# LoRA products of the RWKV group in one pass over 96 stacked rows, issued before the norm of kk

## What is computed

```
p = p + (token_shift(p) - p) * mu
r, k, v, wl, al = jnp.split(p, [G, 2 * G, 3 * G, 3 * G + L], axis=-1)
decay = jnp.exp(-RWKV_DECAY_SCALE * jax.nn.sigmoid(w0 + jnp.tanh(wl) @ w2))
a = jax.nn.sigmoid(a0 + al @ a2)
kk = (k * k_k).reshape(B, T, H, N).astype(jnp.float32)
kk = kk / jnp.maximum(jnp.sqrt(jnp.sum(kk * kk, axis=-1, keepdims=True)), 1e-12)
k = k * (1.0 + (a - 1.0) * k_a)
```

## Time and profile before

| what | value |
|---|---|
| median of 3 runs | 624.18 us (623.57 to 624.37) |
| the profiled execution, its own time | 624.2 us |
| its span in the trace | 622.4 us |
| PE busy | 596.7 us, 96% |
| DVE busy | 377.6 us, 61% |
| ACT busy | 263.9 us, 42% |
| POOL busy | 248.6 us, 40% |

### The profile page before, as it was taken

One profiled execution on the slowest core, in us unless ns is written; L12 is line 12 of the kernel. 1 busy time (PEld: TensorE's weight loads), 2 busy tenths in 40 slices (PEclk: granted clock), 3 DMA queues, 4 the chain that ended last, 5 costly groups with the idle time before them and its releaser, 6 DMA issues.

```text
span 622.4 us, 11997 instructions
## 1 busy us (share of the span) xinstructions
PE 596.7 (96%) x4915; PEld 478.6 (77%) x4915; DVE 377.6 (61%) x642; ACT 263.9 (42%) x509; POOL 248.6 (40%) x192
## 2 busy tenths in 40 slices
PE   3999999999999999999989999999998999999994
PEld 3777878887877777878878787888786777787884
DVE  3858977471358457773275897746224846778433
ACT  4474432423155455533348443242314545644321
POOL 3564534413812223546506364431561313334720
PEclk9999999999999999999999999999999999999998
DMA  7948542526322121355443333252732212135403
GB/s 235 275 115 251 170 102 68 111 29 162 104 68 70 36 69 47 89 187 139 148 119 84 92 97 103 72 107 44 179 82 57 70 35 70 35 95 183 127 1 135
DMA packets 118711, 66.26 MB, mean 106 GB/s; under 512 B 29246, under 2 KB 111746, under 8 KB 118530
## 3 DMA queue, kind: packets, MB, share of 16 engines
q1 hardware_dynamic: 118658, 65.51, 38.5%
HBM read 55.26 MB, written 10.24 MB: 105 GB/s over the span
## 4 chain that ended last, share of the span: by engine, by line
PE 91%; DVE 3%; DMA 2%; issue 1%; ACT 1%; SPq 0%; POOL 0%; DVEq 0%; ACTq 0%; POOLq 0%
PE bank L704 25%; PE bank L707 23%; PE bank L706 23%; PE bank L808 2%; PE bank L878 2%; PE bank L905 2%; DMA pages<-in_x_dram 2%; PE bank L889 2%; PE bank L863 1%; PE bank L823 1%; PE bank L990 1%; PE bank L1025 1%; PE bank L837 1%; PE bank L1041 1%; PE bank L788 1%
## 5 line engine op out<-in xcount | busy, mean ns | idle before, releaser
L636 POOL TENSOR_TENSOR w_lo<-w_raw,w_hi 128x512 fp32r<-128x512 f32 x160 | 222.1, 1411 | 298.1 <-ACT w_hi L1112 298.1
L704 PE MATMUL bank<-act_hi,w_hi 128*128 128x512 f32 x656 | 264.5, 403 | 3.0 <-DVE act_lo L1765 1.3
L707 PE MATMUL bank<-act_lo,w_hi 128*128 128x512 f32 x656 | 256.0, 390 | 0.0
L706 PE MATMUL bank<-act_hi,w_lo 128*128 128x512 f32 x640 | 249.7, 390 | 0.0
L704 PEld LDWEIGHTS bank<-act_hi,w_hi 128*128 128x128 f32 x656 | 123.1, 188 | 40.6 <-issue 13.8
L707 PEld LDWEIGHTS bank<-act_lo,w_hi 128*128 128x128 f32 x656 | 123.1, 188 | 26.5
L706 PEld LDWEIGHTS bank<-act_hi,w_lo 128*128 128x128 f32 x640 | 120.3, 188 | 22.2
L1112 ACT ACTIVATE w_hi<-w_raw 128x512 fp32r<-128x512 f32 (+1 forms) x142 | 80.8, 619 | 52.6 <-PE bank L707 49.5
L1215 ACT ACTIVATE pages<-bank 128x512 f32<-128x512 f32 x24 | 14.3, 597 | 89.3 <-PE bank L707 89.3
L628 POOL TENSOR_TENSOR w_hi<-w_raw,constants 128x512 fp32r<-128x512 f32 (+1 forms) x22 | 22.5, 1042 | 48.2 <-DMA w_raw<-in_w_in_dram 44.6
L1776 DVE TENSOR_TENSOR x_or_y<-x_or_y,bank 128x512 f32<-128x512 f32 x16 | 11.0, 687 | 38.9 <-PE bank L707 38.9
(11 more groups left out here) (188 smaller groups left out, 749.5 us busy)
## 6 DMA issues: line engine op xcount, KB each, us to landing
w_raw<-in_w_in_dram SPq DMA_DIRECT2D x64, 512.0 KB, 4.1
w_raw<-in_w_out_dram SPq DMA_DIRECT2D x16, 512.0 KB, 3.8
x_scratch<-x_or_y SPq DMA_DIRECT2D x16, 256.0 KB, 4.1
x_or_y<-x_scratch SPq DMA_DIRECT2D x16, 256.0 KB, 2.8
pages<-in_x_dram SPq DMA_DIRECT2D x4, 512.0 KB, 9.0
out_dram<-pages SPq DMA_DIRECT2D x4, 512.0 KB, 3.9
bias_scratch<-pages SPq DMA_DIRECT2D x1, 1280.0 KB, 7.4
constants<-in_consts_dram SPq DMA_DIRECT2D x1, 1064.5 KB, 5.8
```

Of the source, the lines that this page charges most:

```text
L636: ins = pool.tensor_tensor(low, w_raw[:, i % RAW, k, 0:n], w_hi[:, i % HI, k, 0:n].bitcast(F32), ALU.subtract)
L704: mm(b[:, :], hi, act_hi[:, k, :], start=n == 0, stop=False)
L706: mm(b[:, :], lo, act_hi[:, k, :], start=False, stop=False)
L707: ins = mm(b[:, :], hi, act_lo[:, k, :], start=False, stop=n == KT - 1)
```

## The change

The LoRA inputs are split into high and low parts on 32-row blocks and stacked over 96 rows of `stat_hi`: for the decay (index 0) high, low, high; for `a` (index 1) high, high, low. The weights are stacked to match, once, in the prologue on VectorE (`lora_parts`, six instructions of 32x512). Each LoRA product is then one fp32r matmul over 96 rows. The stacking of the inputs is a tanh and four copies on ScalarE and two subtractions on VectorE. The steps `lora_input` and `lora` stand before `kk_input`, `decay_scan` before `kk_norm`, and `kk_norm` before `shift v0`.

```diff
-    s += [("shift", "k0"), ("shift", "k1"), ("kk_input",), ("shift", "wa"), ("shift", "r0"), ("kk_square",),
-          ("kk_norm",), ("lora_tanh",), ("shift", "r1"), ("lora",), ("shift", "v0"), ("decay_scan",), ("shift", "v1"),
+    s += [("shift", "k0"), ("shift", "k1"), ("shift", "wa"), ("lora_input",), ("shift", "r0"), ("lora",),
+          ("kk_input",), ("shift", "r1"), ("kk_square",), ("decay_scan",), ("kk_norm",), ("shift", "v0"), ("shift", "v1"),
...
                 def lora():
-                    pe.wait_ge(*at("lora_in", layer))
+                    if layer == 0:
+                        pe.wait_ge(s("lora_ready"), 6)
+                    pe.wait_ge(*at("lora_high", layer))
+                    pe.wait_ge(*at("lora_low", layer))
...
-                            end(mm(b[:, :], lora_w[r0:r0 + LORA, layer, p * P:(p + 1) * P], WA[r0:r0 + LORA, :], start=True, stop=True), f"{z}{p}", layer)
+                            end(mm(b[:, :], lora_r[:, x, layer, p * P:(p + 1) * P], stat_hi[0:3 * LORA, x, :], start=True, stop=True), f"{z}{p}", layer)
...
                 def kk_input():
                     for p in range(2):
                         act.wait_ge(*read(f"k{p}", layer))
-                        if layer > 0:
-                            act.wait_ge(*full(f"var{p}", layer - 1))
+                        act.wait_ge(*full("za1", layer))
...
-                def lora_tanh():
+                def lora_input():
                     act.wait_ge(*at("wa_mixed", layer))
-                    go(WA[0:LORA], WA[0:LORA], ACT.Tanh).then_inc(s("lora_in"), 1)
+                    go(WA[0:LORA], WA[0:LORA], ACT.Tanh).then_inc(s("lora_tanh"), 1)
+                    for p in range(2) if layer > 0 else ():
+                        act.wait_ge(*full(f"var{p}", layer - 1))
+                    go(stat_hi[LORA:2 * LORA, 1, :], WA[LORA:2 * LORA], ACT.Copy).then_inc(s("lora_high"), 1)
+                    act.wait_ge(*at("lora_tanh", layer))
+                    go(stat_hi[0:LORA, 0, :], WA[0:LORA], ACT.Copy).then_inc(s("lora_high"), 1)
+                    go(stat_hi[0:LORA, 1, :], WA[LORA:2 * LORA], ACT.Copy).then_inc(s("lora_high"), 1)
+                    go(stat_hi[2 * LORA:3 * LORA, 0, :], WA[0:LORA], ACT.Copy).then_inc(s("lora_high"), 1)
...
                     dve.tensor_copy(mean_r[:, :], head_mean).then_inc(s("mean_r"), 1)
+                    lora_parts()
+
+                def lora_parts():
+                    first, second, third = (slice(LORA * n, LORA * (n + 1)) for n in range(3))
+                    for x, r, hi, again, lo in ((0, first, first, second, third), (1, second, second, third, first)):
+                        raw = lora_w[r]
+                        dve.tensor_copy(lora_r[hi, x], raw).then_inc(s("lora_ready"), 1)
+                        dve.tensor_copy(lora_r[again, x], raw).then_inc(s("lora_ready"), 1)
+                        dve.wait_ge(s("lora_ready"), 3 * x + 1)
+                        tt(lora_r[lo, x], raw, lora_r[hi, x].bitcast(F32), ALU.subtract).then_inc(s("lora_ready"), 1)
...
+                def lora_input():
+                    for n, (x, r, to) in enumerate(((1, slice(LORA, 2 * LORA), slice(2 * LORA, 3 * LORA)), (0, slice(0, LORA), slice(LORA, 2 * LORA)))):
+                        dve.wait_ge(*at("lora_high", layer, n + 1))
+                        tt(stat_hi[to, x, :], WA[r], stat_hi[r, x, :].bitcast(F32), ALU.subtract).then_inc(s("lora_low"), 1)
```

More of the change, by code:

```diff
@@ L364, in trunk_kernel @@
         mean_r = sb("head_mean_r", [P, P], F32R)
+        lora_r = sb("lora_split_w", [3 * LORA, 2, DEPTH, G], F32R)
         def page(i, n=1):
@@ L431, in trunk_kernel @@
             "h_raw": KT, "h_hi": KT, "h_split": KT,
-            "kk_sq": 2, "kk_unit": 2, "lora_in": 1, "decay_sum": 2,
+            "kk_sq": 2, "kk_unit": 2, "lora_tanh": 1, "lora_high": 4, "lora_low": 2, "decay_sum": 2,
             "decay_exp": 4, "beta": 1, "kappa": 1, "alpha": 3, "rho": 3, "rkv": 2, "pads": 1, "blocks_done": 1, "blocks_turned": 1, "ret_prefix": 1, "conv_tap": 2, "ln_scaled": 2, "ln_affine": 2,
@@ L776, in kk_square @@
                     if layer == 0:
-                        pe.wait_ge(s("const_b"), 16 * 4)
                         pe.wait_ge(s("mean_r"), 1)
@@ L783, in lora @@
                 def lora():
-                    pe.wait_ge(*at("lora_in", layer))
+                    if layer == 0:
+                        pe.wait_ge(s("lora_ready"), 6)
+                    pe.wait_ge(*at("lora_high", layer))
+                    pe.wait_ge(*at("lora_low", layer))
                     for p in range(2):
-                        for z, r0 in (("zw", 0), ("za", LORA)):
+                        for x, z in enumerate(("zw", "za")):
                             b = begin(f"{z}{p}", layer)
-                            end(mm(b[:, :], lora_w[r0:r0 + LORA, layer, p * P:(p + 1) * P], WA[r0:r0 + LORA, :], start=True, stop=True), f"{z}{p}", layer)
+                            end(mm(b[:, :], lora_r[:, x, layer, p * P:(p + 1) * P], stat_hi[0:3 * LORA, x, :], start=True, stop=True), f"{z}{p}", layer)
                 def bonus():
@@ L1348, in project_out @@
                         go(small[:, 24:25], const("eps")[:, 0:1], ACT.Sqrt)
-                run = dict(norm=norm, shift=shift, kk_input=kk_input, kk_norm=kk_norm, lora_tanh=lora_tanh, lora=lora, factors=factors,
+                run = dict(norm=norm, shift=shift, kk_input=kk_input, kk_norm=kk_norm, lora_input=lora_input, lora=lora, factors=factors,
                            decay_exp=decay_exp, gate=gate, copy=copy, to_rows=to_rows,
@@ L1779, in project_out @@
                             evacuate_row(n)
-                run = dict(norm=norm, shift=shift, kk_input=lambda: stat_low("kk", KN), ret_low=lambda: stat_low("ret", RSQ),
+                run = dict(norm=norm, shift=shift, lora_input=lora_input, kk_input=lambda: stat_low("kk", KN), ret_low=lambda: stat_low("ret", RSQ),
                            ln_square=lambda: stat_low("ln", LNS), kk_norm=kk_norm, decay_scan=decay_scan, factors=factors, bonus=bonus,
```

## The result

The changed kernel takes 648.26 us (median of 4 executions, 647.88 to 648.44), the kernel before on the same chip 623.88 us (623.03 to 624.37): the ratio is 1.0392, 95% interval 1.0374 to 1.041. It is slower, as forecast, but by 24.4 us, where the prediction had 11.8 and ended its range at 640.5.

What follows compares the result with a forecast made beforehand. TensorE, busy 96% of the span at full clock, was taken as the bound. Saving and waits together delay rwkv_g0 by 5.6 us in layer 1 and 6.2 in layer 0: 624.2 + 5.6 + 6.2 = 636.0 us, range 632.5 to 640.5.

Steps and rivals of the forecast that it cites:

- the releasers it named: ScalarE's copies end the wait ahead of the LoRA products; VectorE's shift ends the one ahead of rwkv_g0.
- The saving, 1.2 us a layer: TensorE's four LoRA products a layer: single pass takes 0.91 us instead of 2.11, saving 2.4 us in all.
- The rival that 96 rows cost as much as before: LoRA products: fp32r over 96 rows still takes 2.1 us, so the time is 638.4 us; chance 0.02.
- The LoRA inputs, 2.0 us in layer 1: TensorE waits 2.0 us ahead of layer 1's LoRA products, due at 337.54, started at 339.5 behind ScalarE's copies.
- drain behind the table load: ScalarE ahead of tanh: the table load drains, 1.38 us more a layer, giving 638.8 us; chance 0.02.
- The wait at rwkv_g0: TensorE waits about 4.3 us a layer for bank 0, until VectorE's shift of v0.
- VectorE's chain, from r1's shift to v0's: Behind r1's shift stand decay_scan, 5.07 us, and kk_norm, 9.10; with both shifts 15.6 us.
- The weight instructions, 3.5 us: Six on VectorE ahead of layer 0's k0 shift: four casts 1.7 us, two subtractions 0.9 each; sum 3.5.
- the stated upper bound, 5.3: Upper bound for the six weight instructions on VectorE in layer 0; it gives 637.8 us in total.
- The clock, 0 to 4.3 us, rival at 0.28: Clock falls in the rwkv_g0 waits, costing over 1 us each, at most 2.2: 638 to 640.5 us; chance 0.28.
- the wait at rwkv_g0 did not hide (627.2): Rival: no bank wait at rwkv_g0, only the LoRA input wait: 627.2 us; chance 0.1, including everything up to the forecast.
- neither did both (621.8): Rival: LoRA input wait and rwkv_g0 wait both hidden, only the saving shows: 621.8 us; chance 0.03.

Runs made afterwards that it cites:

- experiment 6: Kernel before with the changed kernel's list of steps, full-precision LoRA products kept on their old inputs: 640.86 us, ratio 1.0271.
- 7: Kernel before plus the six weight instructions on VectorE at the changed kernel's place, their result unread: 630.76 us, ratio 1.0109.
- experiment 5: Kernel before with the LoRA products as single-pass fp32r over 96 rows of other stored data, no splitting, decay and a wrong: 621.03 us, ratio 0.9953.
- experiment 4: Changed kernel with both early weight instructions and kk_norm, then v0's shift, ahead of decay_scan: 633.95 us, ratio 1.0155.
- Experiment 1: Changed kernel with the six weight instructions moved ahead of the derived parameters, into VectorE's idle stretch: 644.17 us, ratio 1.0324.
- experiment 3: Changed kernel plus 18 unused products a layer on TensorE ahead of rwkv_g0: 641.95 us, ratio 1.0286.
- experiments 2: Changed kernel with kk_norm, then v0's shift, ahead of decay_scan on VectorE: 639.51 us, ratio 1.0248.
- Experiments 8: Kernel before with single-pass LoRA products issued behind v0, weight casts on ScalarE, inputs' low parts on GpSimd, weight subtractions early on VectorE: 623.32 us, ratio 0.9988.
- 9: The kernel of Experiments 8 with VectorE's two kk products moved behind r1's shift: 622.44 us, ratio 0.998.
- 10: The kernel of experiment 4 plus seven unused products on TensorE ahead of the LoRA products: 632.54 us, ratio 1.0144.

## Why the prediction was right in direction and short by half

The mechanism held: the waits are where the prediction put them, with the releasers it named. What failed is the size of two terms above all. The six weight instructions stand in the sum at 3.5 us, with their casts at 0.43, and took 7.0 beside GpSimd. The falls of the clock stand in it at nothing, and took 6.1 in this trace. Two smaller terms add 3.2. Each follows with its number.

**The sum of the parts.** The order alone costs 16.8 us (experiment 6), the weight instructions alone 6.7 (7), the single pass alone gains 3.0 (5): 20.5 of the 24.4. The other 3.9 come only with all together. The parts hold falls of the clock and late waits that differ between executions (experiments 4 and 5), so each may be off by 1 or 2 us; that is an estimate, from the differences of 0.8 us in a late wait and 2.1 us at the boundary. What is in none of the three is the split of the inputs, and the wait of 2.28 us for it in layer 1 is the largest thing in it; the rest was not measured apart.

**The saving, 1.2 us a layer: right for the products.** In the kernel after the four last 1.16 and 1.21, which is four starts 0.26 to 0.27 apart, a little over the pace forecast; experiment 5 has 0.23 and saves 1.21 a layer on them. What it lacks is v1's bank, which takes 0.3 of it back there; in the kernel after r1's shift stands ahead of the reciprocal on VectorE, so v1 has no such gap. The rival that 96 rows cost as much as before is out.

**The LoRA inputs, 2.0 us in layer 1: the wait is there, 2.28.** What was mis-sized is the pitch of ScalarE's copies. The prediction took 0.52 from the 128-row weight copies; the timeline of ScalarE in the kernel after, layer 0, shows them 0.66 apart:

```profile
44.75 1.28 ACT L1176 ACT_TABLE_LOAD   x1
46.04 0.63 ACT L1176 ACTIVATE pages<-pages 32x512 f32<-32x512 f32 x1
46.70 0.63 ACT L1179 ACTIVATE stat_hi<-pages 32x512 fp32r<-32x512 f32 x1
...
48.67 0.63 ACT L1183 ACTIVATE stat_hi<-pages 32x512 fp32r<-32x512 f32 x1
```

Four such steps make 0.6 us a layer: on the time scale of before the products of layer 1 start at 354.77 - 14.77 = 340.0 (14.77 is how much later ScalarE's first scaling of that layer stands, 342.74 against 327.97), where the prediction had 339.5. There is no drain behind the table load (46.04 is 44.75 + 1.29), so that rival is out too.

**The wait at rwkv_g0: right place, right releaser, 4.51 and 5.68 instead of 4.3.** VectorE's chain, from r1's shift to v0's, in layer 1 after:

```profile
362.19 0.75 DVE L1483 SCALAR_TENSOR_TENSOR pages<-bank,params,pages 128x511 f32<-128x511 f32 x1 [0.17 <-ACT pages L1157]
362.85 1.80 DVE L1510 TENSOR_SCALAR pages<-pages 128x1024 f32<-128x1024 f32 x1
364.68 3.31 DVE L1512 TENSOR_TENSOR_SCAN pages<-constants,pages 128x512 f32<-128x512 f32 x2
367.92 0.66 DVE L1502 TENSOR_SCALAR pages<-pages 128x1024 f32<-128x1024 f32 x1
368.62 6.55 DVE L1503 RECIPROCAL pages<-pages 128x1024 f32<-128x1024 f32 x1
375.20 3.40 DVE L1505 SCALAR_TENSOR_TENSOR pages<-pages,params 128x512 f32<-128x512 f32 x2
378.53 1.39 DVE L1483 SCALAR_TENSOR_TENSOR pages<-bank,params,pages 128x511 f32<-128x511 f32 x2
```

From 362.85 to 378.53 are 15.68 us, where the prediction had 5.07 + 9.10 = 14.17. All of the 1.5 lies in the two kk products, 375.20 to 378.53, 3.33 us from start to start, instead of 9.10 - 0.70 - 6.58 = 1.82: GpSimd works on two weight halves from 375.12 to 378.06. In layer 0 they take 2.42 and the chain 14.70, 0.5 over. The term was a row of the same instructions, but the row was read where GpSimd was idle: in the kernel before, its block ends at 345.45 + 2.54 = 347.99, and the kk products start at 348.39.

**The weight instructions, 3.5 us: 7.0.** This is the largest miss of a single term. The prediction's 0.43 for a cast is right where GpSimd is idle; it allowed for GpSimd in the subtractions only, and too little. Experiment 1 shows the step: the same six take 3.2 us four microseconds earlier. Even the stated upper bound, 5.3, took its casts at 0.43.

**The clock, 0 to 4.3 us, rival at 0.28: it fell, and more often than counted.** Behind the two waits at rwkv_g0 it cost 1.7 and 2.3 us, as the rival said; experiment 3 shows both as the price of the wait. It fell in r0's wait of layer 0 too, from 39.3 to 46.1, but there it cost nothing of its own: the split inputs were ready at 48.67 + 0.63 = 49.30, and the products started at 49.40. What nobody had listed is the layer boundary. The profiled execution of the kernel before has the same waits there of 0.57 and 0.66 and keeps the full clock; after, a window of it reads:

```profile
326.00:328.00 2.00, 1.43 (x7) 1.42 (x7) 0.18 (x1) 0.26 (x1) 0.00 (x0) 0.50 0.91 208
```

In the kernel after, whose four executions have 0.975 to 0.977, the delay against before grows there from 80.41 - 67.73 = 12.7 (ScalarE's first row from rwkv_g0 of layer 0) to 14.8 (its first scaling in layer 1): 2.1 us. The Trainium skill, "TensorE: Matmul & The Clock Gate", section "HAM oscillation — how this bites in real kernels", lays such falls to long idle gaps. For the waits at rwkv_g0 the trace agrees; at the boundary the idle times are under 0.7 us and the same in both kernels, so by that rule nothing should have happened there. Why the clock falls there in the traces of the kernel after and of experiments 2, 4 and 6, and not in those of 1, 3, 5, 7 to 10 or before, stays open. I have no run that moves the boundary alone. Nor is it shown that the change brings this fall. Executions of one kernel differ: of fifteen of the kernel before on one chip, five have a mean granted clock of 0.989 to 0.992 and take 623.2 to 625.8 us, ten have 0.993 to 0.996 and take 622.6 to 624.4. Half clock all the way from the last matmul to the end would make (622.4 - 614.1) / 2 = 4.2 us, a mean of 0.993. So those five had a fall somewhere else too, which the profiled execution, at 0.995, doesn't have.

**The sum of the misses.** 3.5 (weights) + 1.2 (copies) + 2.0 (kk products beside GpSimd) + 1.7 + 2.3 + 2.1 (clock) = 12.8, less 1.0 that is given back between 387 us and the last matmul. That makes 11.8; the span missed by 11.9 (23.7 against 11.8). Of the 1.0, 0.8 is in waits that the trace gives to no other engine (in all 2.4 us before and 1.6 after, late in layer 1); what ends them was not looked into. The largest is the one at L971 and L975 (experiment 5).

**The rivals that ended below:** the wait at rwkv_g0 did not hide (627.2), and neither did both (621.8). Experiments 8 and 9 show one way to a gain: with the order of before, and the splitting on engines that are idle then, the waits shrink enough to leave 1.4 us. Of the versions run that compute all that the kernel must, only these two come out below the kernel before.

## What to carry to other kernels

Where TensorE hardly ever waits, as here, a saving in matmul slots (2.4 us) can be small beside what its new operands and their order cost (over 20): look first for the time at which the splitting and copying can lie in an idle stretch of VectorE and ScalarE, and ask of each step that is moved which bank's reader now stands behind it. Take the price of a VectorE instruction from a row with the same neighbour on GpSimd, not only with the same shape. And put a price on every new wait of TensorE twice, once for the wait and once for the slow matmuls behind it (here 1.7 to 2.3 us for waits of 4.5 to 5.7). Before a difference of 1 or 2 us between two traces is laid to an edit, look at the mean granted clock of all executions of both kernels.

## What the hardware showed that was not expected

- Casts of 32x512 took 0.41 with GpSimd idle and 1.37 beside its subtractions, subtractions of that size 0.68 and 1.65, the kk products (a row by source, durations in ns) 0.75 and 1.75:

```profile
L1505 DVE SCALAR_TENSOR_TENSOR pages<-pages,params x4: 750/1736/1753, 69.8 to 376.9; 128x512 f32<-128x512 f32 x4
```

- In the RWKV front parts of these twelve traces the granted clock went to half at all ten waits of TensorE of 4.5 us and more, and at four of the five of 2.27 and 2.28 (experiments 1 to 4, not the kernel after, at 354.77). At the layer boundary, with waits of 0.57 and 0.66, it did so in four of the twelve. One kernel's executions differ in it (experiment 4: 0.987 to 0.995).
- With products added that nobody reads the kernel ran 6.3 us faster (experiment 3); rwkv_g0 took 1.6 and 2.1 us less by the traces, and a fall elsewhere in layer 1 took the second back.
- ScalarE's copies of 32 rows follow each other without overlap, 0.66 apart at 0.63 each, where the weight copies of 128 rows start 0.52 apart.
